# First panels behind a norm multiplied input block by input block, and normalised blocks handed over one at a time

## The reference, cut to what matters

```python
def rms_norm(x, g):
    y = xf * lax.rsqrt(jnp.mean(xf * xf, axis=-1, keepdims=True) + EPS)
    return (y * g.astype(jnp.float32)).astype(x.dtype)

x = x + gated_branch_mixer(rmsnorm(x, norm_mix_g[l]), ...)          # norm "mix"
x = x + memory_cross_attention(rmsnorm(x, norm_x_g[l]), ...)        # norm "x"
x = x + hierarchical_moe(rmsnorm(x, norm_ffn_g[l]), ...)            # norm "ffn"
...
h = rms_norm(x, ln_mix_g[i]) * (1.0 + sc1) + sh1                    # "n" (i=0), "d" (i=1)
y = nsa_mixer(h, ...)   or   diff_mixer(h, ...)
h = rms_norm(x, ln_mlp_g[i]) * (1.0 + sc2) + sh2                    # "m0", "m1"
x = x + g2 * (jnp.square(jax.nn.relu(h @ w_mlp_in[i])) @ w_mlp_out[i])
```

## Time and profile before

| what | value |
|---|---|
| median of 3 runs | 1523.8 us (1523.14 to 1527.52) |
| profiled execution, its own time | 1521.02 us |
| its span in the trace | 1518.4 us |
| PE busy, share of the span | 1448.5 us, 95% |
| DVE, ACT busy | 964.1 us, 627.4 us |
| mean granted PE clock, share of full | 0.968 |

### The profile page before, as it was taken

The page is one execution under the profiler, slowest core; times in us unless marked ns, Lnnn a source line. Parts: engine busy times, 40 slices in busy tenths (PEclk is TensorE's granted clock), DMA queues, the critical chain, the costliest instruction groups (busy, mean ns, idle before and its releaser), DMA issues.

```text
span 1518.4 us, 26270 instructions
## 1 busy us (share of the span) xinstructions
PE 1448.5 (95%) x11023; PEld 1367.0 (90%) x11023; DVE 964.1 (63%) x1205; ACT 627.4 (41%) x793; POOL 65.7 (4%) x111
## 2 busy tenths in 40 slices
PE   7999999999999999989998999899989998999998
PEld 6999999889999999988986578899989876899998
DVE  5679877545677667666416856788774476555453
ACT  5444453444443333444512644334444325344441
POOL 4030000000000000000000000000000000000000
PEclk9999999999999999999968999999999989999999
DMA  8555543433588887854510024999963420256551
GB/s 230 192 181 194 165 141 124 160 118 125 190 285 267 272 273 252 275 167 133 179 49 0 2 79 147 315 305 309 311 223 109 156 84 1 84 168 192 180 181 56
DMA packets 173573, 260.92 MB, mean 172 GB/s; under 512 B 5509, under 2 KB 148147, under 8 KB 173363
## 3 DMA queue, kind: packets, MB, share of 16 engines
q1 hardware_dynamic: 160890, 203.13, 41.3%
q0 software_dynamic: 10128, 51.30, 10.0%
q10 hardware_dynamic: 2472, 5.31, 1.1%
HBM read 258.67 MB, written 1.05 MB: 171 GB/s over the span
## 4 chain that ended last, share of the span: by engine, by line
PE 81%; DVE 11%; ACT 3%; issue 2%; DMA 2%; SPq 1%; ACTq 0%; DVEq 0%
PE ring L635 60%; PE acc L635 19%; DVE arena L1707 1%; DVE w_lo L1661 1%; ACT arena L1209 1%; ACT w_hi L1209 1%; DVE arena L1799 1%; PE acc L1045 1%; PE ring L892 1%; DVE h_lo L1701 1%; DVE norm L1676 1%; DMA raw<-in_w_mlp_in_dram 1%; DMA vec_in<-in_nsa_pe_v_dram 1%; DVE arena L2180 1%; DVE arena L2177 0%
## 5 line engine op out<-in xcount | busy, mean ns | idle before, releaser
L1661 DVE TENSOR_TENSOR w_lo<-raw,w_hi 128x2048 fp32r<-128x2048 f32 (+1 forms) x191 | 437.0, 2289 | 338.3 <-ACT w_hi L1209 338.1
L635 PE MATMUL ring<-h_hi,w_hi 128*128 128x256 f32 x2088 | 598.5, 287 | 10.6 <-DVE h_lo L1701 7.3
L635 PE MATMUL ring<-h_lo,w_hi 128*128 128x256 f32 x2088 | 592.8, 284 | 0.0
L635 PE MATMUL ring<-h_hi,w_lo 128*128 128x256 f32 x2088 | 592.6, 284 | 0.0
L1209 ACT ACTIVATE w_hi<-raw 128x2048 fp32r<-128x2048 f32 (+1 forms) x191 | 363.4, 1903 | 241.8 <-DMA raw<-in_w_mlp_out_dram 66.8
L635 PEld LDWEIGHTS ring<-h_hi,w_hi 128*128 128x128 f32 x2088 | 402.4, 193 | 18.0 <-DVE h_lo L1701 7.4
L635 PEld LDWEIGHTS ring<-h_lo,w_hi 128*128 128x128 f32 x2088 | 402.4, 193 | 0.5
L635 PEld LDWEIGHTS ring<-h_hi,w_lo 128*128 128x128 f32 x2088 | 402.2, 193 | 0.0
L635 PE MATMUL acc<-e_hi,w_hi 128*128 128x256 f32 x768 | 219.6, 286 | 2.2 <-DVE e_lo L2306 2.1
L635 PE MATMUL acc<-e_lo,w_hi 128*128 128x256 f32 x768 | 218.2, 284 | 0.0
L635 PE MATMUL acc<-e_hi,w_lo 128*128 128x256 f32 x768 | 218.1, 284 | 0.0
(11 more groups left out here) (261 smaller groups left out, 1362.6 us busy)
## 6 DMA issues: line engine op xcount, KB each, us to landing
arena<-in_w_ada_dram POOLq DMA_DIRECT2D x64, 768.0 KB, 5.8
raw<-in_w_mlp_in_dram SPq DMA_DIRECT2D x32, 1024.0 KB, 5.5
raw<-in_w_mlp_out_dram SPq DMA_DIRECT2D x32, 1024.0 KB, 5.1
raw<-in_w_in_dram SPq DMA_DIRECT2D x24, 1024.0 KB, 5.2
raw<-in_w_e_gate_dram SPq DMA_DIRECT2D x16, 1024.0 KB, 5.6
raw<-in_w_e_up_dram SPq DMA_DIRECT2D x16, 1024.0 KB, 6.4
raw<-in_w_e_down_dram SPq DMA_DIRECT2D x16, 1024.0 KB, 5.7
raw<-in_diff_w_in_dram SPq DMA_DIRECT2D x12, 1024.0 KB, 5.1
```

Of the source, the lines that this page charges most:

```text
L635: return nc.tensor.matmul(dst, lhs, rhs, start=start, stop=stop, **kw)
L1661: tt(w_lo[q % SPL][:, 0:n], raw[q % RAW][:, 0:n], w_hi[q % SPL][:, 0:n].bitcast(F32), ALU.subtract)\
```

## The change

On PE, a new `linear_first` takes one or two panels. It opens all of them first, and then goes through the input blocks: for each k it waits for one block of h and does all that the block feeds (both output blocks of each panel, 6 matmuls a panel). mix, x, n and d use it for their first two panels, ffn, m0 and m1 for one. On DVE and ACT, scaled, hi and ready now count single blocks, and the order in `split_norm` is another. The places of `ahead` and the counts of `keep_busy` stay.

```diff
-        PER_NORM = {"squared": 4, "summed": 1, "scaled": 4, "hi": 4, "ready": 4}
+        PER_NORM = {"squared": 4, "summed": 1, "scaled": KB, "hi": KB, "ready": KB}
...
+            def linear_first(panels, f, ready):
+
+
+                for i in range(len(panels)):
+                    open_panel(panels[i])
+                    open_fill(f + i)
+                for k in range(KB):
+                    ready(k)
+                    for i, p in enumerate(panels):
+                        wh = w_hi[p % SPL][:].rearrange("p (k n) -> p k n", k=KB)
+                        wl = w_lo[p % SPL][:].rearrange("p (k n) -> p k n", k=KB)
+                        for b in range(2):
+                            o, c = bank(f + i)[:, b * T:(b + 1) * T], slice(b * P, (b + 1) * P)
+                            mm(o, wh[:, k, c], h_hi[:, k, :], k == 0 and b == 0, False, skip_group_check=True)
+                            mm(o, wh[:, k, c], h_lo[:, k, :], False, False, skip_group_check=True)
+                            last = mm(o, wl[:, k, c], h_hi[:, k, :], False, k == KB - 1, skip_group_check=True)
+                        if k == KB - 1:
+                            last.then_inc(S("panel_done"), 1)
...
-            full("a_gate", h_ready("mix_ready"))
+            full("a_gate", split="mix_ready")
...
-            pe.wait_ge(*sig("ffn_scaled", 4))
+            pe.wait_ge(*sig("ffn_scaled", KB))
...
-            ready = h_ready("ffn_ready")
-            linear(PN["moe"], moe_fill(0), KB, 2, lambda k: h_hi[:, k, :], lambda k: h_lo[:, k, :], ready)
+            linear_first([PN["moe"]], moe_fill(0), block_ready("ffn_ready"))
...
-                def low(j):
-                    dve.wait_ge(*sig(tag + "_hi", j + 1))
-                    s = slice(2 * j, 2 * j + 2)
+                def low(b):
+                    dve.wait_ge(*sig(tag + "_hi", b + 1))
                     if shift is None:
-                        last = tt(h_lo[:, s, :], blk(mid, 8)[:, s], h_hi[:, s, :].bitcast(F32), ALU.subtract)
+                        last = tt(h_lo[:, b, :], blk(mid, 8)[:, b], h_hi[:, b, :].bitcast(F32), ALU.subtract)
...
-                for j in range(KB // 2):
-                    for b in (2 * j, 2 * j + 1):
-                        last = stt(blk(mid, 8)[:, b], x_t[:, b, :], gain(b), norm[:, row, :], ALU.mult, ALU.mult)
-                    last.then_inc(S(tag + "_scaled"), 1)
-                    if j:
-                        low(j - 1)
-                low(KB // 2 - 1)
+                for b in range(KB):
+                    stt(blk(mid, 8)[:, b], x_t[:, b, :], gain(b), norm[:, row, :], ALU.mult, ALU.mult)\
+                        .then_inc(S(tag + "_scaled"), 1)
+                    if b == 1:
+                        low(0)
+                    elif b > 2:
+                        low(b - 2)
+                low(KB - 2)
+                low(KB - 1)
```

More of the change, by code:

```diff
@@ L691, in h_ready, with block_ready, ready, full @@
                 return ready
-            def full(name, ready=None, norm=None):
-                for i in range(FL_N[name]):
+            def block_ready(sem):
+                def ready(k):
+                    pe.wait_ge(*sig(sem, k + 1))
+                return ready
+            def full(name, ready=None, norm=None, split=None):
+                if split is not None:
+                    linear_first([PN[name], PN[name] + 1], FL[name], block_ready(split))
+                for i in range(2 if split is not None else 0, FL_N[name]):
                     linear(PN[name] + i, FL[name] + i, KB, 2, lambda k: h_hi[:, k, :], lambda k: h_lo[:, k, :],
@@ L795, in _ @@
             keep_busy(FL["x_q"], 10)
-            full("x_q", h_ready("x_ready"))
+            full("x_q", split="x_ready")
             def x_scores(h):
@@ L919, in _ @@
             keep_busy(FL["n_q"], 21)
-            full("n_q", h_ready("n_ready"))
+            full("n_q", split="n_ready")
             full("n_kc")
@@ L1099, in mlp @@
                 keep_busy(FL[name], 11)
-                linear(PN[name], FL[name], KB, 2, hi, lo, h_ready(f"m{l}_ready"))
+                linear_first([PN[name]], FL[name], block_ready(f"m{l}_ready"))
                 def chunk_step(c):
@@ L1125, in _ @@
             keep_busy(FL["d_q"], 11)
-            full("d_q", h_ready("d_ready"))
+            full("d_q", split="d_ready")
             full("d_k")
@@ L1241, in high_parts @@
             def high_parts(tag, hh, src, shift=None):
-                for j in range(KB // 2):
-                    act.wait_ge(*sig(tag + "_scaled", j + 1))
+                for b in range(KB):
+                    act.wait_ge(*sig(tag + "_scaled", b + 1))
                     if shift is None:
-                        func(hh[:, 2 * j:2 * j + 2, :], src[:, 2 * j:2 * j + 2], ACT.Copy).then_inc(S(tag + "_hi"), 1)
+                        func(hh[:, b, :], src[:, b], ACT.Copy).then_inc(S(tag + "_hi"), 1)
                     else:
-                        for b in (2 * j, 2 * j + 1):
-                            last = func(hh[:, b, :], src[:, b], ACT.Identity, bias=shift(b))
-                        last.then_inc(S(tag + "_hi"), 1)
+                        func(hh[:, b, :], src[:, b], ACT.Identity, bias=shift(b)).then_inc(S(tag + "_hi"), 1)
             def norm_act(tag, ready, shift=None, before=None):
@@ L1284, in _ @@
             ahead(PN["a_val"])
-            act.wait_ge(S("mix_ready"), 4)
+            act.wait_ge(S("mix_ready"), KB)
             squares_of("mem", blk(MEM_T, 8), blk(SQ, 8), lambda j: drained_wait(act, FL["mem_t"] + j))
@@ L1453, in _ @@
             ahead(PN["n_q"])
-            act.wait_ge(*sig("n_ready", 4))
+            act.wait_ge(*sig("n_ready", KB))
             act.dma_start(flat(SPREAD, 0, 12 * P), a["k_spread_rows"][:, 0:12 * P]).then_inc(S("spread_landed"), 16)
@@ L1692, in split_norm @@
                 chain.settle()
-                def low(j):
-                    dve.wait_ge(*sig(tag + "_hi", j + 1))
-                    s = slice(2 * j, 2 * j + 2)
+                def low(b):
+                    dve.wait_ge(*sig(tag + "_hi", b + 1))
                     if shift is None:
-                        last = tt(h_lo[:, s, :], blk(mid, 8)[:, s], h_hi[:, s, :].bitcast(F32), ALU.subtract)
+                        last = tt(h_lo[:, b, :], blk(mid, 8)[:, b], h_hi[:, b, :].bitcast(F32), ALU.subtract)
                     else:
-                        for b in (2 * j, 2 * j + 1):
-                            last = stt(h_lo[:, b, :], blk(mid, 8)[:, b], shift(b), h_hi[:, b, :].bitcast(F32),
-                                       ALU.add, ALU.subtract)
+                        last = stt(h_lo[:, b, :], blk(mid, 8)[:, b], shift(b), h_hi[:, b, :].bitcast(F32), ALU.add, ALU.subtract)
                     last.then_inc(S(tag + "_ready"), 1)
-                for j in range(KB // 2):
-                    for b in (2 * j, 2 * j + 1):
-                        last = stt(blk(mid, 8)[:, b], x_t[:, b, :], gain(b), norm[:, row, :], ALU.mult, ALU.mult)
-                    last.then_inc(S(tag + "_scaled"), 1)
-                    if j:
-                        low(j - 1)
-                low(KB // 2 - 1)
+                for b in range(KB):
+                    stt(blk(mid, 8)[:, b], x_t[:, b, :], gain(b), norm[:, row, :], ALU.mult, ALU.mult)\
[6 more added lines that the diff above has]
+                low(KB - 1)
             def lows(src, hi, lo, sem_hi, sem_ready, shift=None, nb=KB):
```

## The result

The changed kernel takes 1517.3 us (median of 13 runs, 1513.19 to 1522.25), the kernel before 1526.8 us beside it (13 runs, 1520.26 to 1531.88). The ratio over all runs is 0.9946, 95% interval 0.9931 to 0.9962: 8.2 us won, between 5.8 and 10.5 (the two medians alone are 9.5 us apart). The profiled execution has a span of 1511.3 us where before it was 1518.4, 7.1 less.

What follows compares the result with a forecast made beforehand. PE, busy 95% of the span and 81% of the chain, was taken as the bound; -12.5 at five norms, +0.7 at ffn and +5.3 at mix give -6.5, so 1523.8 becomes 1517.3 us; 8-in-10 range 1511.5 to 1521.5.

Steps and rivals of the forecast that it cites:

- Five norms that win: At x, n, d, m0 and m1 PE goes from keep_busy straight into the product and stands less; 12.5 us won together.
- The fifth panel at n: Its w_lo, delayed by the later panel_done, is split near 714 and needed at 719; hidden with 5 us to spare.
- ffn: Router product waits for all eight scaled blocks, which come later behind single subtractions; 0.7 us lost.
- mix, the wait: PE waits for panel 1's w_lo, split behind the norm; a_gate starts at 27.3 instead of 22.66, 3.6 us lost after mem_t.
- mix, the clock: After the wait at mix, a_gate's matmuls start at the half clock level; 1.7 us lost, bounds 0 and 2.4.
- the dear bound of 2.4: Upper bound of the clock loss at mix: 5.5 us at half level, doing 44% less, costs 2.4 us.
- the row with the nearest length of wait: Earlier trace's 3.9 us wait at 964.3, then 4.0 us at 0.57 clock; used to price mix's clock at 1.7 us.
- regained at mem_t: Behind a_gate at mix, ACT's table load already delayed the drain, so 0.6 us of the loss is got back.
- The wait costs nothing lasting: Rival: four DVE waits between 174 and 262 us take up mix's delay; sum -8 to -12 us; 12 in 100.
- The gains come half: Rival: 40 waits in the five norms cost 0.1 us each even when satisfied; time 1519 to 1522; 20 in 100.
- The clock falls in the new loop: Rival: half clock in the two-panel products from alternating banks, 8.6 us a product, making the kernel slower; 5 in 100.
- Single panels win only 1.5: Rival: at m0 and m1 DVE is the bound, winning 1.5 instead of 2.3 us; time 1519, inside the forecast.

Runs made afterwards that it cites:

- experiment 10: The changed kernel with all four panels of n_q in one pass of the new loop instead of two; one run, 1516.9 us.
- experiment 1: The changed kernel with the w_lo of panel 1 made ahead of the norm mix instead of behind it; 1515.1 us, ratio 0.9934 to before.
- experiment 2: The changed kernel with a_gate at mix multiplied panel by panel again, blocks still handed over singly; 1511.9 us, ratio 0.9905 to before.
- experiment 7: The changed kernel with mix's panel 1 w_lo made ahead of the norm and all eight ffn scalings before the subtractions; 1510.4 us, ratio 0.9904 to before.
- experiment 8: The changed kernel with 20 instead of 6 matmuls of keep_busy ahead of a_gate at mix; one run, 1523.4 us.
- experiment 5: The changed kernel with PE's old order in all seven places, keeping only the single-block handover; 1524.9 us, ratio 1.0001 to before.
- experiment 4: The kernel before with linear_first at a_gate (mix) alone, blocks handed over in pairs as before; 1530.8 us, ratio 1.003 to before.
- experiment 6: The kernel before with linear_first at all seven norms, blocks still handed over in pairs; 1519.3 us, ratio 0.9961 to before.
- experiment 3: The changed kernel with 16 instead of 6 matmuls of keep_busy ahead of a_gate at mix; 1520.5 us, ratio 0.9962 to before.
- 9: The changed kernel with the new loop over one panel instead of two at mix, x, n and d; 1515.9 us, ratio 0.9945 to before.
- 11: The changed kernel with a_gate at mix panel by panel and all ffn scalings before the subtractions; 1511.3 us, ratio 0.9913 to before.

## Why the prediction was right

The sum of the seven norms was forecast at 6.5 us and is 6.56 in the trace. The mechanism at each norm was right; that the sum agrees so closely is partly luck, as the clock terms show. By its own steps:

- **Five norms that win: 12.5 forecast, 13.1 measured.** The first product starts right behind keep_busy in all five. At the two-panel norms matmuls run at 0.12 us without a stop, 97 in 11.4 us at x. At m0 and m1 PE follows DVE at 0.80 us a block (0.8 forecast), and the panel ends 8.3 us after the first scaling (8.4). These stages repeat: x, m0, d and m1 agree within 0.02 us in eight traces that have the changed kernel's program there, n within 0.4 in seven.
- **The fifth panel at n** was said to have 5 us to spare. w_lo was ready 5 us ahead, and with four panels in the loop (experiment 10) the cover was gone and the wait there.
- **ffn: 0.7 forecast, 0.82 measured.** The gap before the router grew from 0.62 to 1.28 us, as the sum had it, and 0.66 is the part that repeats: the router starts 7.91 us behind the start of keep_busy in experiments 1 and 2 too. The rest is clock, and by the clock alone the stage takes 19.83 to 22.04 us in the seven traces with this program at ffn. The router's 0.62 us of before was there to be won too; experiment 7 took it.
- **mix, the wait: right.** a_gate was to start at 27.3, released by w_lo; it started at 27.18. Counted from keep_busy's start it came 4.7 us later than before.
- **mix, the clock: direction right, size 1.7 forecast, about 2.5 in this trace** (against a_gate without a wait in experiment 8), just over the dear bound of 2.4. The step that doesn't hold is the way to the price. I took it from the row with the nearest length of wait; after this wait of 4.16 us half clock held for 5.8 us, but behind 5.49 us in experiment 10, with the same program at mix, it cost only 1.3 us, and five waits for w_lo here cost 1.3 to 2.6 us in no order of their lengths (last section). The forecast of 1.7 lies between. In this trace the excess was offset by more regained at mem_t: 4.71 + 2.26 (a_gate 14.23 us instead of 11.97) - 5.76 = 1.2 us, where 0.6 was forecast. The Trainium skill (TensorE: Matmul & The Clock Gate, section HAM oscillation — how this bites in real kernels) says that matmuls behind a long wait begin cold. Here the trace agrees: 27 of 96 matmuls at half clock behind the wait, none without it. Of the 1.94 us wait in experiment 1 it holds as well (0.51 for 3.4 us), while behind 2.0 us at 950 us in the earlier trace rows and behind 2.60 us in experiment 5 the clock stayed full.
- **The rivals.** *The wait costs nothing lasting*: fell, the four waits are unchanged and experiment 4 lost 0.3% by mix alone. *The gains come half*: fell, satisfied waits on single blocks cost nothing that the 0.12 us pace shows. *The clock falls in the new loop*: fell, 1.00 at x over the whole loop and in experiment 8. The rule of the Trainium skill on bank cycling (same page, section A second HAM failure mode: psum-queue depth-cycling) does not bite here: going between two banks every six matmuls kept the full clock. *Single panels win only 1.5*: fell, they won 2.49 each.

The time against before fell by 8.2 us where the sum said 6.5; the interval (5.8 to 10.5) holds both. That the predicted and the measured median are both 1517.3 is partly luck: the forecast started from 1523.8 and the runs beside the changed kernel had 1526.8. And between the norms a loss of 1.7 us (d to m1), which the forecast did not have, met a gain of 1.8 us (n to m0) that comes and goes.

## What to carry to other kernels

Where a producer hands over blocks and the consumer waits, change the handover and the order of the consumer together: either alone gave 0.4 or 8.5 us of 13.1. Before a loop is widened over several panels, look at each place for what it now needs earlier (here the second w_lo, at mix alone) and what it frees later (here the slot of the fifth panel, at n), for one exception of seven ate 5.8 of the 13.1 us. And a wait of a few us in front of TensorE can cost more than its length, since the work behind it may run at half clock: 1.3 to 2.6 us more at mix behind waits of 1.9 to 6.9 us, but nothing behind 2.60 us in experiment 5. Price it as a range.

## What the runs showed of the hardware

**What a wait costs in clock isn't set by its length.** a_gate has the same loop and the same 96 matmuls in all these traces (in experiments 4 and 6 it waits for pairs of blocks). The times are starts in the timelines:

| trace | PE idle ahead of a_gate, us | a_gate to mem_t, us | more than without a wait |
|---|---|---|---|
| experiments 7 and 8 | 0 | 11.70 | 0 |
| experiment 1 | 1.94 | 13.08 | 1.4 |
| after | 4.16 | 14.23 | 2.5 |
| experiment 3 | 4.51 | 13.08 | 1.4 |
| experiment 4 | 4.79 | 13.97 | 2.3 |
| experiment 10 | 5.49 | 13.03 | 1.3 |
| experiment 6 | 6.86 | 14.25 | 2.6 |

In the old order the clock stayed full behind waits of 2.60 us (experiment 5) and 1.43 us (experiment 2). What decides the price was not found.

**Half clock in the attention stage differs from one execution to the next.** The stretch of PE from 740 to 912 us (columns as above), in the traces of before, after, experiment 6 and experiment 8, in this order:

```profile
740.00:912.00 172.00, 160.59 (x1099) 129.06 (x1098) 92.28 (x229) 68.49 (x186) 1.05 (x2) 0.86 0.16 51
```

```profile
740.00:912.00 172.00, 160.65 (x1114) 128.13 (x1114) 93.82 (x230) 68.92 (x186) 1.04 (x2) 0.87 0.17 56
```

```profile
740.00:912.00 172.00, 160.78 (x1029) 127.40 (x1028) 87.48 (x223) 65.23 (x183) 1.05 (x2) 0.80 0.14 47
```

```profile
740.00:912.00 172.00, 160.12 (x1033) 127.22 (x1032) 89.43 (x226) 63.92 (x182) 1.05 (x2) 0.81 0.13 43
```

PE is as busy in all four, but the granted clock is 0.80 to 0.87 and the matmuls done in the same time are 1029 to 1114. By length, the stage from n to m0 took 177 us in the changed kernel, 188 in experiment 6 and 187 in experiment 8 (176.8 to 181.3 in all the others). Experiment 8 is a kernel whose program differs from the changed one only in a count at mix, 700 us earlier. Ten us of difference between two executions come from here, which is more than the whole change. A single span can't judge such a change, and experiment 6's span of 1527.0 with a ratio of 0.9961 is the example. What makes an execution take one course or the other was not found.

**The same twelve matmuls at mix took 5.33 us or 2.75.** keep_busy ran at half clock in before and in after, at full clock in experiments 1, 2, 5 and 6, and partly so in 4 (4.38 us), 7 and 9 (4.44), 10 (4.00) and 11 (4.13). PE's idle time just ahead, in which it waits for a small transfer (vec_in), was 2.91 us in before, 2.99 in after, 2.80 in 7, 2.61 in 4 and 11, 2.28 in 10, and 2.20, 1.82, 1.63 and 0.45 in 1, 6, 2 and 5, but 2.10 in 9. So a longer wait mostly goes with the lower clock, and its length alone doesn't decide it. No experiment took this wait by itself. It matters for the stage: where keep_busy took 2.75 us, PE then stood for h or w_lo (1.43 to 6.86 us).
